# Stick-breaking attention: the triangular sums as two single-pass products on split softplus values

## The reference

```python
def _stick_breaking_block(qb, kb, vb, start):
    z = jnp.einsum('bhqd,bhkd->bhqk', qb, kb)
    nq = qb.shape[2]
    nk = kb.shape[2]
    visible = jnp.arange(nk)[None, :] < (start + jnp.arange(nq))[:, None]
    log_keep = jnp.where(visible, jax.nn.log_sigmoid(-z), 0.0)
    later = lax.cumsum(log_keep, axis=3, reverse=True) - log_keep
    w = jnp.where(visible, jnp.exp(jax.nn.log_sigmoid(z) + later), 0.0)
    return jnp.einsum('bhqk,bhkd->bhqd', w, vb)
```

## Time and profile before

| | |
|---|---|
| median of 3 runs | 1445.28 us (1445.23 to 1447.59) |
| the profiled execution | 1443.03 us |
| its span | 1441.3 us |
| busy in the span | PE 93%, DVE 46%, ACT 36%, POOL 39% |
| the attention | about 176 to 253 us |
| L867 in the chain that ended last | 1% of the span, L865 as much |

### The profile page before, as it was taken

The page is one execution under the profiler, slowest core; times in us unless marked ns, Lnnn a source line. Parts: engine busy times, 40 slices in busy tenths (PEclk is TensorE's granted clock), DMA queues, the critical chain, the costliest instruction groups (busy, mean ns, idle before and its releaser), DMA issues.

```text
span 1441.3 us, 21128 instructions
## 1 busy us (share of the span) xinstructions
PE 1334.8 (93%) x9266; PEld 1181.7 (82%) x9266; DVE 659.9 (46%) x957; ACT 513.5 (36%) x678; POOL 569.2 (39%) x200
## 2 busy tenths in 40 slices
PE   6997798797999999999879999998979999999995
PEld 5997665797999999999769888877658888888873
DVE  7996944457431013414272564464574400344145
ACT  4324377434222222222263344354342311322222
POOL 2343054165333344444553222244643443344350
PEclk9998899998999999999989999999989999999997
DMA  5221000121233332333211111112112332333311
GB/s 173 90 88 60 2 2 1 43 76 59 89 88 89 95 103 96 88 88 89 88 57 61 59 59 59 59 59 88 59 59 88 114 90 88 100 105 88 92 55 59
DMA packets 142044, 108.22 MB, mean 75 GB/s; under 512 B 8096, under 2 KB 139376, under 8 KB 141952
## 3 DMA queue, kind: packets, MB, share of 16 engines
q1 hardware_dynamic: 141552, 106.77, 24.3%
q10 hardware_dynamic: 400, 0.11, 0.0%
HBM read 104.77 MB, written 2.10 MB: 74 GB/s over the span
## 4 chain that ended last, share of the span: by engine, by line
PE 75%; DVE 15%; ACT 5%; issue 2%; POOL 2%; DMA 1%; SPq 0%; DVEq 0%; POOLq 0%; ACTq 0%
PE pb L592 60%; DVE h L1821 2%; PE pb L650 2%; PE pb L652 2%; PE pb L651 2%; PE pb L660 2%; DVE h L1807 1%; PE pb L867 1%; DVE bc L1867 1%; DVE h L1792 1%; POOL sqs L480 1%; PE pb L865 1%; DMA x_tok<-in_x 1%; DVE st L1906 1%; POOL wl L464 1%
## 5 line engine op out<-in xcount | busy, mean ns | idle before, releaser
L464 POOL TENSOR_TENSOR wl<-raw,wh 128x2048 fp32r<-128x2048 f32 x97 | 452.0, 4660 | 651.2 <-ACT wh L1061 651.2
L592 PE MATMUL pb<-hh,wh 128*128 128x264 f32 (+1 forms) x1376 | 360.0, 321 | 31.1 <-ACT hh L1317 19.9
L592 PE MATMUL pb<-hh,wl 128*128 128x264 f32 (+1 forms) x1376 | 353.1, 315 | 0.0
L592 PE MATMUL pb<-hl,wh 128*128 128x264 f32 (+1 forms) x1376 | 347.0, 314 | 0.8 <-POOL hl L496 0.6
L592 PEld LDWEIGHTS pb<-hh,wh 128*128 128x128 f32 x1376 | 229.7, 192 | 54.0 <-issue 26.9
L592 PEld LDWEIGHTS pb<-hh,wl 128*128 128x128 f32 x1376 | 229.0, 191 | 15.3
L592 PEld LDWEIGHTS pb<-hl,wh 128*128 128x128 f32 x1376 | 225.9, 189 | 17.4 <-POOL hl L496 1.6
L592 PE MATMUL pb<-hidh,wh 128*128 128x264 f32 (+1 forms) x768 | 205.3, 322 | 3.5 <-POOL wl L464 3.5
L592 PE MATMUL pb<-hidh,wl 128*128 128x264 f32 (+1 forms) x768 | 203.3, 319 | 0.0
L592 PE MATMUL pb<-hidl,wh 128*128 128x264 f32 (+1 forms) x768 | 202.8, 318 | 0.0
L1061 ACT ACTIVATE wh<-raw 128x2048 fp32r<-128x2048 f32 x97 | 185.0, 1907 | 1.4 <-DMA raw<-in_w_in_c 1.4
(11 more groups left out here) (348 smaller groups left out, 1631.4 us busy)
## 6 DMA issues: line engine op xcount, KB each, us to landing
raw<-in_mlp_w_up SPq DMA_DIRECT2D x32, 1024.0 KB, 5.4
raw<-in_mlp_w_down SPq DMA_DIRECT2D x32, 1024.0 KB, 5.7
raw<-in_w_in_c SPq DMA_DIRECT2D x16, 1024.0 KB, 5.5
raw<-in_w_in_ab SPq DMA_DIRECT2D x8, 1024.0 KB, 5.7
raw<-in_w_out_ab SPq DMA_DIRECT2D x4, 1024.0 KB, 5.1
raw<-in_w_out_c SPq DMA_DIRECT2D x4, 1024.0 KB, 5.2
x_tok<-in_x SPq DMA_DIRECT2D x2, 1024.0 KB, 7.7
out_h<-o_tok SPq DMA_DIRECT2D x4, 512.0 KB, 3.1
```

The source lines that it names most:

```text
L464: pool.tensor_tensor(wl[:, c % RING, :], raw[:, c % RING, :], wh[:, c % RING, :].bitcast(F32), ALU.subtract).then_inc(w_lo, 1)
L592: mm = pe.matmul(pb[:, bank + b, 0:z_ - a], lhs, rhs[:, a:z_], start=first and hi and k == 0, stop=last and k == len(todo) - 1)
```

## The change

The ntri product of each unit is replaced by two products of float32r operands: ntri_r (a float32r copy of the triangular matrix, made once by ACT) times sph and times spl. sph is sp rounded to float32r, spl is sp - sph; DVE makes both right behind soft(g), in four buffers each (g % 4), so that soft now waits from g = 4 on for acc of unit g - 4. In acc the nones products come first and the two ntri_r products last, behind a wait for the split (sp_split). The ntri product of the 16 meta tokens (acc0) stays as it is.

```diff
--- before.py
+++ after.py
@@
+        ntri_r = sb("ntri_r", [P, P], F32R, m0b)
@@
+        sph = sb("sph", [P, 4, 512], F32R, m0b)
+        spl = sb("spl", [P, 4, 512], F32R, m0b)
@@
-            pe.wait_ge(mask_r, 3)
+            pe.wait_ge(mask_r, 4)
@@
-                pe.matmul(pb[:, n, 0:UNIT[s]], ntri[:, :], sp[:, n, 0:UNIT[s]], start=False, stop=False, skip_group_check=True)
                 if s == 0:
                     later(144, 160, sa[:, 0:16], False)
                     later(416, 432, sa[:, 0:16], False)
-                    mm = later(288, 432, sa[:, 16:160], True)
+                    later(288, 432, sa[:, 16:160], False)
                 elif s == 1:
                     later(128, 256, sa[:, 160:288], False)
                     pe.wait_ge(later_ready, 4 * i + hd + 1)
-                    mm = later(256, 400, lb[:, hd, :], True)
+                    later(256, 400, lb[:, hd, :], False)
                 else:
                     later(112, 240, sb_[:, 0:P], False)
                     pe.wait_ge(later_ready, 4 * i + hd + 3)
-                    mm = later(240, 512, lc[:, hd, :], True)
+                    later(240, 512, lc[:, hd, :], False)
+                pe.wait_ge(sp_split, g + 1)
+                for part, x_ in enumerate((sph, spl)):
+                    mm = pe.matmul(pb[:, n, 0:UNIT[s]], ntri_r[:, :], x_[:, g % 4, 0:UNIT[s]], start=False, stop=part == 1,
+                                   skip_group_check=True)
                 mm.then_inc(acc_ready, 1)
@@
+                    act.activation(ntri_r[:, :], ntri[:, :], ACT.Copy).then_inc(mask_r, 1)
@@
-                if g >= 6:
+                if g >= 4:
                     dve.wait_ge(acc_ready, g - 3)
                 STT(sp[:, n, 0:c], pb[:, n, 0:c], 0.0, al[:, g % 2, 0:c], ALU.max, ALU.add).then_inc(sp_ready, 1)
+                dve.wait_ge(sp_ready, g + 1)
+                dve.tensor_copy(sph[:, g % 4, 0:c], sp[:, n, 0:c]).then_inc(sp_high, 1)
+                dve.wait_ge(sp_high, g + 1)
+                TT(spl[:, g % 4, 0:c], sp[:, n, 0:c], sph[:, g % 4, 0:c].bitcast(F32), ALU.subtract).then_inc(sp_split, 1)
```

More of the change, by code:

```diff
@@ L327, in trunk @@
         later_ready = sem("later_ready")
+        sp_high = sem("sp_high")
+        sp_split = sem("sp_split")
         acc_ready = sem("acc_ready")
```

## The result

The changed kernel takes 1453.27 us, the median of 5 runs (1451.16 to 1453.7), beside 1446.57 us for five runs of the kernel before on the same chip. The ratio is 1.0044 with a 95% interval from 1.003 to 1.0059, so the slowdown is real, if small. The forecast was 1455.2 us with a range from 1448.5 to 1460. As a change it was +9.9 us; the medians differ by 6.7.

What follows compares the result with a forecast made beforehand. The chain of waits bounds the attention, through ACT in half a round and PE in the crossings. Crossings 8.1, tail 0.4 and clock 1.4 make 9.9 us on the 1445.28 median: 1455.2 us, range 1448.5 to 1460.

Steps and rivals of the forecast that it cites:

- the crossings: Three attention stretches, acc with s=2, hd=1 to the head pair's last pv_pair; DVE-POOL port waits add 8.1 us.
- the tail: Behind unit 23, at the attention's end: split, pair and pv pairs take 0.4 us more.
- the clock: PE's clock falls after idle time, for the last pair and its pv_pair, in one of three crossings: +1.4 us.
- The added instructions: DVE's CAST and subtraction per unit, 1.0 to 1.1 us alone, some 25 us in all, fitting DVE's idle time.
- The ones products as cover: In acc, the unchanged ones products now run first while DVE splits, hiding some 0.7 us of its work.
- the pv pairs 2.1: Behind unit 23, the pv pairs were to take 2.1 us, ending at 252.9 to 253.3.
- (a): In the crossings, DVE keeps the port between its own instructions: no difference, say 1446 us; 7%.
- (b): New DVE instructions hardly meet POOL; each crossing 0.9 us shorter, 2.8 in all, 1442.5 us; 7%.
- (c): POOL locks the port for the whole instruction, L535 and L539 included: 3.6 us more, 1458.8 us; 6%.
- POOL now done: At a crossing's end, CAST and subtraction of unit 13 meet no POOL work and end at 222.74.
- (d): The clock falls in every crossing: 4.3 us instead of 1.4, 1458.1 us; 15%.
- (e): Weights hold up single-pass products, so the pair saves nothing: 0.4 us more a crossing; inside the range, no own chance.

Runs made afterwards that it cites:

- The split alone: Changed kernel with the old float32 ntri product in front; DVE splits but nobody reads the parts: 1451.3 us, ratio 1.0039.
- the order alone: Kernel before with the float32 ntri product last in acc, no split: 1445.25 us, ratio 1.0003.
- The filled kernels: Changed kernel plus dummy products in PE's idle time, units 11, 17, 23: 1450.62 us (1.004); also units 13, 19: 1450.92 us (1.0045).
- the short gelu: Five of POOL's seven gelu instructions on 16 columns, two memsets: changed kernel 1440.53 us (0.9965), kernel before 1445.33 us (1.0002).
- the products alone: Changed kernel without split: softplus sum written as float32r, ntri_r product run twice on it: 1436.46 us, ratio 0.9935.
- the early gate: ACT's gelu gate at n = 2 instead of n = 4: kernel before 1440.07 us (0.9968), changed kernel 1448.19 us (1.0022).

## Why the prediction was right, and which terms were off

**The mechanism and its place** came out as forecast. The chain in the crossings goes through DVE, the subtraction takes up to 1.94 us (forecast: up to 2.2) inside and 0.6 to 0.7 outside, PE's products wait for DVE, POOL's instructions are stretched, and the ends of the rounds still wait for PE. The split alone is slower, and without POOL's work the change is a gain.

**The sum** came out by errors that partly cancel. Forecast: 8.1 in the crossings, 0.4 in the tail, 1.4 for the clock, 9.9 in all. In the profiles it is 8.1: 5.98 in the crossings with the clock's share in them, 1.76 in the tail, 0.16 elsewhere in the attention, 0.89 behind it and -0.70 outside. By the medians it is 6.7, two thirds of the forecast. That 1455.2 lies within 2 us of 1453.27 is in part luck: the forecast stood on a median of 1445.28 for the kernel before, and its five runs have 1446.57.

**The crossings** were forecast at +8.1 us and measured 1.63 + 2.24 + 2.11 = 6.0. This is the mis-sized term. In the second crossing DVE's schedule from the softplus sum of unit 11 to the subtraction of unit 13 took 224.14 - 215.96 = 8.18 us where I had 9.22. I let POOL hold the port for the whole length of its TENSOR_TENSOR records (1.57, 1.07, 1.31), but each hold was some 0.3 us shorter, 0.85 us in all. (The hold is counted from the end of DVE's instruction before it to the end of the delayed one, less that one's own length; it ends 0.13 to 0.15 us ahead of POOL's record.) In part the shortfall was offset: my 0.44 us from the split to pv_pair allowed the pair its cost in a stream of products (0.39, at 223.54), and behind a wait it takes 0.66 (at 205.07). And in the second crossing PE itself came late, since pv_pair(4) and z_pair(7) ran at half clock (1.53 and 1.60 us; 0.82 and 0.88 at full), so that the pair of unit 13 started at 224.62, not at 224.18, but then ran in a stream. The third crossing had the clock at 1.00 and was only 0.14 us shorter.

**The added instructions**: the CAST 0.42 and 0.38 us forecast, 0.43 and 0.38 measured uncontended; the subtraction 0.69 and 0.61, measured 0.69 and 0.61. The pair 0.40 in a stream, measured 0.39.

**The ones products as cover, and the order**: the order alone measures 1.0003, as costed.

**The tail and the clock.** I had +0.4 us for the tail and +1.4 for a fall of the clock in one crossing of three. The tail gave +1.76: the split ends 2.42 us behind the softplus sum (forecast 2.70), but the pair and the eight v products take 1.22 + 3.24 = 4.46 us, all at half clock, where I had 2.6 to 3.0. The filled kernels run the same at 0.74 + 1.76 us. So the step "the pv pairs 2.1" failed: I took over the time of work in whose middle the clock had come back, and behind the new wait on the split it came back only after it. The products behind the attention pay too, 12.64 us for the first 96 instead of 11.75. In the crossings the clock fell in one of three, as the count assumed, but in the middle, and cost 0.14 us there instead of 1.4. The price itself was right for a fall that lasts over the last pair: the filled kernel paid 1.33 us. Tail and clock together, 1.8 forecast, are 1.9 in the attention and 0.9 behind it, so two wrong terms made a nearly right sum.

**Outside the attention**, forecast at nothing: it starts 0.6 us later (kernels without the added copy of ntri start anywhere from 177.7 to 179.4), and 1.3 us are won back behind 1200 us. Neither can be put down to the change.

**The rivals.** No handing over (a) and faster (b) are refuted by the 1.93 and 1.40 us of the DVE rows. Rival (b) was right on one thing: where DVE doesn't wait, a round gets shorter (16.5 us with the short gelu: forecast 0.9 us less than before, measured 0.55 less). Rival (c), the lock for the whole instruction, would have had L1697 wait for all of L544 (until 223.25), and it was done at 222.38: for this instruction the port was again free after some 0.5 us. For a CAST it was not: that of unit 13 (222.94) took 0.56 us instead of 0.38 while L544 still ran, and so it was in all three crossings. My schedule had "POOL now done" there. The Trainium skill (SBUF — State Buffer, "Who interferes with whom") states the lock for the whole instruction; the rows agree for POOL's TENSOR_TENSOR, whose hold ends 0.13 to 0.15 us before its record, and for the CAST behind L544, but not for DVE's TENSOR_TENSOR beside POOL's TENSOR_SCALAR. Rival (d), the clock falling in each crossing, is not what happened: it fell in the second, not in the third. (e), no gain from the pair, is refuted by 0.39 us for 432 columns and by the rounds of 15.98 us of the products alone.

**What stays open**: what decides where the clock falls in a kernel, and the part of what the products alone and the short gelu gain in the medians, but not in their profiled executions.

## What to carry to other kernels

Before moving work to DVE, look at what POOL does at that very time, and price each added instruction by its contended duration: the same added DVE work was a gain of some 5 us with POOL's instructions cut short, and a loss of 7 beside them. When a critical stretch changes its engine, the gain on the old one is gone: the products alone bring 9 us, the split alone costs 5, together they cost 7. Moving POOL's block was a small edit and brought the old kernel 5 us, but it has to go where DVE has nothing to do that shares the port: in the changed kernel it met the split again.

## What the hardware showed that I had not expected

- A float32 to float32r CAST from SBUF to SBUF runs at 0.37, 0.39 and 0.43 us for 400, 432 and 512 columns, faster than the subtraction (0.57, 0.61, 0.69), but it waits for POOL (up to 0.855 us, with the early gate 1.77), beside a TENSOR_SCALAR of POOL too, which let a TENSOR_TENSOR of DVE through after 0.5 us. The longer form with an input in PSUM didn't wait once in 24 times (0.681 at most).
- The same idle time does not always bring the clock down. Around 217 to 219 us PE was busy 0.57 us in 2 and the clock was 0.50 from 219 on; from 236 to 238 it was busy 0.52 us in 2 and the clock stayed at 1.00. In the tail it stayed at 0.50 for over 5 us of busy PE (from 256.9 on).
- Two products that follow a wait took 0.66 us, the same two in a stream 0.39.
- DVE's demand slows POOL as well, by 0.2 to 0.45 us for an instruction (L550, L538).
